# Two memory attentions of a two-block transformer kernel: probabilities normalised by GpSimd before they are turned, values stationary in the weighing

## The reference, cut to what matters

```python
def memory_attention(mq, mk, mv):
    sc = jnp.einsum('bshd,bmhd->bhsm', mq, mk, preferred_element_type=jnp.float32) * (MEM_HEAD_DIM ** -0.5)
    p = jax.nn.softmax(sc, axis=-1)
    out = jnp.einsum('bhsm,bmhd->bshd', p.astype(mv.dtype), mv)
    return out.reshape(B, S, MEM_W)
...
        mo = memory_attention(mq, mk, mv)
        x = x + jnp.concatenate([mixed, mo], axis=-1) @ w_out[l]
```

## Time and profile before

| what | value |
|---|---|
| median of 3 runs | 3211.76 us (3211.11 to 3211.96) |
| the profiled execution's own time | 3211.97 us |
| its span, first to last instruction | 3210.2 us |
| mean granted TensorE clock | 0.998 |
| PE busy | 3160.4 us, 98% |
| DVE busy | 1786.2 us, 56% |
| ACT busy | 1143.9 us, 36% |
| POOL busy | 430.5 us, 13% |

### The profile page before, as it was taken

How to read it: one execution, slowest core, us unless ns; L and a number is a source line. 1 busy time by engine, 2 the same in 40 slices (tenths; PEclk the granted TensorE clock), 3 DMA queues, 4 the chain that set the end, 5 groups by cost and what they waited for, 6 DMA issues and landing times. The chain is left out here.

```text
span 3210.2 us, 41446 instructions
## 1 busy us (share of the span) xinstructions
PE 3160.4 (98%) x15754; PEld 2584.8 (81%) x15754; DVE 1786.2 (56%) x1932; ACT 1143.9 (36%) x1331; POOL 430.5 (13%) x335
## 2 busy tenths in 40 slices
PE   8999999999999999999999999999999999999998
PEld 6778888877788888888877888888888877878887
DVE  7875635459653445534586754345444577664344
ACT  4553212259332222322343433223322343533221
POOL 0002000110100025000253120003000154120002
PEclk9999999999999999999999999999999999999999
DMA  4212232322122224232221122324223221122222
GB/s 158 83 47 99 92 105 92 107 96 83 69 92 92 95 101 122 89 108 92 92 80 66 62 89 86 105 90 131 92 92 104 79 92 67 53 94 93 102 94 76
DMA packets 46600, 293.45 MB, mean 91 GB/s; under 512 B 5888, under 2 KB 6272, under 8 KB 18336
## 3 DMA queue, kind: packets, MB, share of 16 engines
q1 hardware_dynamic: 44496, 286.97, 25.9%
q0 software_dynamic: 2000, 5.05, 1.0%
HBM read 289.24 MB, written 2.10 MB: 91 GB/s over the span
## 5 line engine op out<-in xcount | busy, mean ns | idle before, releaser
L1925 DVE TENSOR_TENSOR w_lo<-w_raw,w_hi 128x2048 fp32r<-128x2048 f32 (+1 forms) x284 | 667.0, 2349 | 244.1 <-ACT w_hi L1484 243.9
L903 PE MATMUL ps<-xg_hi,w_hi 128*128 128x512 f32 x1920 | 749.6, 390 | 2.2 <-DVE w_lo L1925 2.2
L903 PE MATMUL ps<-xg_hi,w_lo 128*128 128x512 f32 x1920 | 747.1, 389 | 0.0
L903 PE MATMUL ps<-xg_lo,w_hi 128*128 128x512 f32 x1920 | 747.0, 389 | 0.0
L1484 ACT ACTIVATE w_hi<-w_raw 128x2048 fp32r<-128x2048 f32 (+1 forms) x286 | 541.1, 1892 | 461.2 <-PE ps L903 359.5
L903 PE MATMUL ps<-hid_hi,w_hi 128*128 128x512 f32 x1216 | 473.3, 389 | 0.0
L903 PE MATMUL ps<-hid_lo,w_hi 128*128 128x512 f32 x1216 | 473.0, 389 | 0.0
L903 PE MATMUL ps<-hid_hi,w_lo 128*128 128x512 f32 x1216 | 473.0, 389 | 0.0
L903 PEld LDWEIGHTS ps<-xg_hi,w_hi 128*128 128x128 f32 x1920 | 360.4, 188 | 79.2 <-issue 4.8
L903 PEld LDWEIGHTS ps<-xg_lo,w_hi 128*128 128x128 f32 x1920 | 360.5, 188 | 75.8 <-issue 1.4
L903 PEld LDWEIGHTS ps<-xg_hi,w_lo 128*128 128x128 f32 x1920 | 360.4, 188 | 75.3
(11 more groups left out here) (369 smaller groups left out, 3902.4 us busy)
## 6 DMA issues: line engine op xcount, KB each, us to landing
w_raw<-up_dram SPq DMA_DIRECT2D x120, 1024.0 KB, 4.8
w_raw<-in_dram SPq DMA_DIRECT2D x42, 1024.0 KB, 4.9
w_raw<-down_dram SPq DMA_DIRECT2D x32, 1024.0 KB, 4.8
w_raw<-down_dram SPq DMA_DIRECT2D x32, 768.0 KB, 4.2
w_raw<-down_dram SPq DMA_DIRECT2D x32, 640.0 KB, 3.9
w_raw<-out_dram SPq DMA_DIRECT2D x14, 1024.0 KB, 4.8
w_raw<-out_dram SPq DMA_DIRECT2D x8, 768.0 KB, 4.2
w_raw<-memk_dram SPq DMA_DIRECT2D x4, 1024.0 KB, 4.9
```

The costliest lines, as they stand in the source:

```text
L903: last = pe.matmul(to, (w_hi, w_lo)[wp][:, q, t:t + P], parts[xp], start=(k == 0 and m == 0), stop=(k == p.ktiles - 1 and m == 2))
L1925: dve.tensor_tensor(w_lo[:, q, 0:w], w_raw[:, q, 0:w], w_hi[:, q, 0:w].bitcast(F32), ALU.subtract)\
```

## The change

For both memory attentions: DVE takes the reciprocal of unit n+1's row sums at its unit n (`inverse_memory`), POOL multiplies the exponentials by it in place, one instruction per head (`normalise`), and only then does PE turn them. The weighing has the values stationary and the turned probabilities moving (`weigh_memory`), so that its output has features on the partitions; DVE takes `hi` and `lo` from there (`finish_memory`). `turn_out` and the multiplication of `back` are gone for memory units. The near attention of the second block keeps the old steps; only its semaphore counts move. `rec` is one buffer, so the next reciprocal waits until POOL has used the last.

```diff
+WINDOWS = 16
+MEMORIES = 12
...
+        def normalise(u):
+
+            pool.wait_ge(rec_done, u.n + 1)
+            s_ = score_sb(u)
+            for i in range(u.nh):
+                last = pool.tensor_scalar(s_[:, i, :], s_[:, i, :], rec[:, i:i + 1], None, ALU.mult)
+            last.then_inc(norm_done, 1)
...
+        for u in SECTIONS["window"][WINDOWS:]:
+            normalise(u)
+
         for p in PHASES:
+            if p.name == "in1_1":
+                for u in M1:
+                    normalise(u)
...
         def turn_probs(u):
-            pe.wait_ge(exp_done, u.n + 1)
+            if u.kind == "memory":
+                pe.wait_ge(norm_done, u.n + 1 - WINDOWS)
+            else:
+                pe.wait_ge(exp_done, u.n + 1)
...
+        def weigh_memory(u):
+            pe.wait_ge(pt_ready, u.n + 1)
+            pe.wait_ge(ot_ready, u.f)
+            for i in range(u.nh):
+                for kb in range(u.nk):
+                    last = pe.matmul(ps[:, u.o_bank, i * P:(i + 1) * P], u.v[kb][i], turned(u)[:, kb, i * P:(i + 1) * P],
+                                     start=(kb == 0), stop=(kb == u.nk - 1))
+            last.then_inc(o_psum, 1)
...
-                if n and us[n - 1].kind == "memory":
-                    turn_out(us[n - 1])
                 if n in MEM_UNITS:
                     memory_slab(MEM_UNITS.index(n))
                 if u.kind == "window":
                     weigh_window(u)
                 else:
-                    weigh(u)
+                    weigh_memory(u)
...
-            first_out(1, 4, 6)
-            turn_out(us[-1])
-            first_out(1, 6, 8)
+            first_out(1, 4, 8)
...
-                if n:
-                    turn_out(M1[n - 1])
                 if 1 <= n < 7:
                     out_half(n - 1)
-                weigh(u)
+                weigh_memory(u)
             out_half(6)
-            turn_out(M1[-1])
             out_half(7)
...
+        def inverse_memory(u):
+            dve.wait_ge(exp_done, u.n + 1)
+            if u.n > WINDOWS:
+                dve.wait_ge(norm_done, u.n - WINDOWS)
+            dve.reciprocal(rec[:, 0:u.nh], rowsum[:, u.n % 2, 0:u.nh]).then_inc(rec_done, 1)
+
+        def finish_memory(u):
+            dve.wait_ge(o_psum, u.n + 1)
+            o = ps[:, u.o_bank, 0:u.nh * P].rearrange("p (t q) -> p t q", t=u.nh)
+            dve.tensor_copy(u.hi[0], o).then_inc(o_ready, 1)
+            dve.wait_ge(o_ready, u.n + 1)
+            dve.tensor_tensor(u.lo[0], o, u.hi[0].bitcast(F32), ALU.subtract).then_inc(ot_ready, 1)
...
         def attention(us):
...
                 if u.kind == "window":
                     finish_window(u)
                     if us[n + 1].kind == "window":
                         inverse_window(us[n + 1])
+                    else:
+                        inverse_memory(us[n + 1])
                 else:
-                    back(u)
-                    if n and us[n - 1].kind != "window" and us[n - 1].last:
-                        finish(us[n - 1])
+                    if n + 1 < len(us):
+                        inverse_memory(us[n + 1])
+                    finish_memory(u)
...
                 output(n)
+            inverse_memory(M1[0])
             front(M1[1], 1)
             low(DT - 1)
             split(MIX_O + 1)
...
                 if n == 2:
                     split(MIX_O + 2)
-                back(u)
-                if n:
-                    finish(M1[n - 1])
-            finish(M1[-1])
+                if n + 1 < len(M1):
+                    inverse_memory(M1[n + 1])
+                finish_memory(u)
```

More of the change, by code:

```diff
@@ L372, in program @@
     rec_done = sem("rec_done")
+    norm_done = sem("norm_done")
     o_ready = sem("o_ready")
@@ L2154, in finish_window @@
             dve.tensor_tensor(u.lo, o, u.hi.bitcast(F32), ALU.subtract).then_inc(ot_ready, 1)
+        def inverse_memory(u):
[9 more added lines that the diff above has]
+            dve.tensor_tensor(u.lo[0], o, u.hi[0].bitcast(F32), ALU.subtract).then_inc(ot_ready, 1)
         def back(u):
             dve.wait_ge(exp_done, u.n + 1)
+            if u.n == WINDOWS + MEMORIES:
+                dve.wait_ge(norm_done, MEMORIES)
             dve.reciprocal(rec[:, 0:u.nh], rowsum[:, u.n % 2, 0:u.nh]).then_inc(rec_done, 1)
@@ L2173, in finish @@
         def finish(u, between=None):
-            dve.wait_ge(ot_psum, u.f + 1)
+            dve.wait_ge(ot_psum, u.f + 1 - MEMORIES)
             src = ps[:, u.ot_bank, u.ot_col:u.ot_col + u.ntile * P]
[L2177 to L2194, removed]
-        def attention(us):
[L2197 to L2201, removed]
+            parts = [(src[:, t * P:(t + 1) * P], u.hi[t], u.lo[t],
+                      v("na_gain", 4 * (u.nf // NCB) + t)) for t in range(4)]
+            for s_, hi, lo, g in parts:
+                last = dve.tensor_scalar(hi, s_, g, None, ALU.mult)
+            last.then_inc(ot_hi, 1)
+            if between is not None:
+                between()
+            dve.wait_ge(ot_hi, u.f + 1 - MEMORIES)
+            for s_, hi, lo, g in parts:
+                last = dve.scalar_tensor_tensor(out=lo, in0=s_, scalar=g, in1=hi.bitcast(F32), op0=ALU.mult,
+                                                op1=ALU.subtract)
+            last.then_inc(ot_ready, 1)
+        def attention(us):
+            inverse_window(us[0])
             for n, u in enumerate(us):
@@ L2204, in attention @@
                     front(us[n + 2], n + 2)
-                if us is SECTIONS["window"] and n in MEM_AHEAD:
+                if n in MEM_AHEAD:
                     split = MEM_SLAB + MEM_AHEAD[n]
                     split_low(split, split % 2, SLAB_T * P)
-                if us is SECTIONS["window"] and n in MEM_UNITS:
+                if n in MEM_UNITS:
                     memory_slab(MEM_UNITS.index(n))
@@ L2213, in attention @@
                         inverse_window(us[n + 1])
-                else:
-                    back(u)
-                    if n and us[n - 1].kind != "window" and us[n - 1].last:
-                        finish(us[n - 1])
-                if us is SECTIONS["window"] and n in MEM_SPLITS:
+                    else:
+                        inverse_memory(us[n + 1])
+                else:
+                    if n + 1 < len(us):
+                        inverse_memory(us[n + 1])
+                    finish_memory(u)
+                if n in MEM_SPLITS:
                     split = MEM_SLAB + MEM_SPLITS[n]
                     split_low(split, split % 2, SLAB_T * P)
-            finish(us[-1])
         rope_n = [0]
```

## The result

| | before | after |
|---|---|---|
| median | 3211.86 us (3210.29 to 3212.23, 6 runs) | 3237.52 us (3236.12 to 3239.39, 6 runs) |
| the profiled execution's own time | 3211.97 us | 3236.64 us |
| its span | 3210.2 us | 3234.8 us |
| granted TensorE clock, mean | 0.998 | 0.996 |

The changed kernel takes 1.0081 of the time before (95% interval 1.007 to 1.0092): 25.7 us more, where 3.7 were forecast. The sign is the forecast's; the time is 15.7 us past the upper end of its range. The profiled executions alone lie 24.7 us apart.

A forecast was written before the change was run, and what follows sets the result against it. PE, busy in 98% of the span, was taken to bound the kernel. Added waits less removed transposes and waits gave +1.9 us in layer 0 and +1.75 in layer 1: 3211.76 + 3.7 = 3215.5 us, range 3211.5 to 3221.8.

The forecast's parts named there:

- the upper end of its range: 3221.8 us: 0.55 us per POOL head gives +8.0, and one meeting or one clock fall +2.
- Where time passes: In both layers' memory units, PE's turning waits for DVE's reciprocal and POOL's multiplications; the first waits +3.55 and +2.8 us.
- the turning of unit 16: Layer 0: reciprocal behind unit 15's closing, then POOL; turning starts at 231.15, not 227.60, +3.55 us, with no filling.
- The loop of layer 1: Turning to next turning takes 4.13 us against 3.47 of PE's own work: +0.65 in units 2, 4, 5, 6.
- The unit with the split: Layer 1, unit 3: DVE's split of 2.29 us stands between front(4) and its reciprocal, +2.85 us.
- the lower end of the range: 3211.5 us: 0.30 per head gives +2.4, PE's fewer changes between groups -1.2, and 1 us for the layout.
- The removed part: The 32 output transposes on PE, their waits and changeovers: 8 to 10 us gained if nothing took their place.
- POOL's price: POOL's multiplications, per 128x256 head: 0.343 us apart, 0.40 for the last; 1.43 us for 4 heads, 0.74 for 2.
- The rival of long heads: POOL's heads in both stretches take longer, each 0.1 us costing 2.2 us; at 0.69, 3223.2 us. Chance 0.20.
- The meeting with a split: POOL work meeting a DVE low split: counted on the slower side, with +2 for one meeting or clock fall.
- +2: Allowance in us at the range's upper end for one meeting with a split or one clock fall.
- The clock: Rival: PE's clock falls after idling 3.55, 2.8 and 2.85 us in one piece. Chance 0.07, half beyond 0.2%.

The follow-up runs named there:

- e1_two_op: The changed kernel with a second operation, times 1.0, added to POOL's multiplication; 3220.28 us, ratio 1.0028 to the kernel before.
- e9_early_two_op: The changed kernel with DVE's reciprocal of unit n+1 ahead of front(n+2) and POOL's multiplication given a second operation, times 1.0; 3208.47 us.
- e10_short_splits: The changed kernel with the two low splits behind units 16 and 17 cut to 128 of 2048 columns; 3231.76 us.
- e6_own_rec: The changed kernel with memory reciprocals in their own buffer, ahead of front(n+2), and unit 16's ahead of unit 15's closing; 3207.18 us.
- e5_filled_less: The changed kernel with 22, 18, 14, 13 and 14 unread identity products in PE's gaps ahead of five turnings; 3229.75 us.

## Why the prediction was wrong

**Where time passes: right.** The whole price is exposed waiting of PE at the turnings behind the chain scores, front, reciprocal, POOL, and unit 16 has no cover. Put 0.91 for 0.343 into the forecast's own chain and its places come out: the turning of unit 16 at +3.55 and 2.21 (four heads at 3.64 less 1.43), 5.76; measured 233.58 against 227.60, 5.98, of which the stretch began 0.35 late. The loop of layer 1 at 4.13 + 1.08 = 5.21 us; measured 5.23 from 863.84 to 869.07, and 5.59 in the unit before. The unit with the split 4.13 + 2.2 + 1.08 = 7.41; measured 844.31 to 851.73, 7.42. One side sum of the forecast doesn't come out: its own terms for the lower end of the range, +2.4 - 1.2 - 1, give 3212.0 us, not 3211.5. Nothing hangs on it.

**The removed part: right.** 8 to 10 us forecast, 9.3 measured.

**POOL's price: the step that failed.** The forecast said "The nearest rows are the same operation on 512 columns". It was not the same: L725 has two scalars, and the row's name, TENSOR_SCALAR, hides that; the source line shows it. Half of 0.69 was a fair guess for the two-scalar form (0.46 apart measured, 0.11 more), and the row of copies gave the price of a copy, while the form in the diff took 0.92, above the "from above 0.69" that was to bound it. By the forecast's units, 2.21 us for each of units 16 to 18 and 1.08 for each of units 1 to 6 of layer 1 are +13.1 us. The rival of long heads had this mechanism and the right side, at 0.20; it gave 3223.2 us at its 0.69, and its slope of 2.2 us per 0.1 us leads to 3228 at 0.92.

**The meeting with a split: left out, and it came twice.** The forecast's sum, with short heads, holds no meeting, and the upper end of its range allows for one. With long heads POOL's groups of units 17 and 18 both run into a split and take 1.6 us more each, +3.2 us. A head of 0.92 or 0.48 us that began inside a split of 2.28 or 2.40 came out at 2.5 (2.55, and 2.51 in e1_two_op), and no head was longer than 0.93 once the split was short. A head already at work when the split began did not hold the split up: 0.93 and 2.28 us (246.23 and 246.61 above). The "+2" that the range has for one meeting or one clock fall was the author's estimate, and no run shows it as one price; the runs showed 1.6 us for a meeting here (2.0 in e1_two_op, 3.88 less 1.85) and, by the rows, 1.4 to 1.7 for a fall.

**The clock: put at 0.07, and it fell four times.** Gaps of 5.56, 4.49, 3.40 and 3.60 us were followed by turnings and scores slower by, in order, 0.9 + 0.7, 0.2 + 1.5, 0.5 + 0.9 and 0.5 + 0.9 us: 6.1 us by these rows, 7.8 by the filled gaps and medians. The forecast's argument against it, full clock where PE waits now (granted 1.00 from 227 to 262 and from 817 to 853 us of the kernel before), rested on waits of at most 1.2 us in these stretches and said nothing of gaps three times as long. Whether its own gaps of 3.55, 2.8 and 2.85 would have brought a fall is open, but 0.07 was low. In e1_two_op a fall came after 3.77 us at unit 16, and one soon after the turning that ended a gap of 2.71 us in layer 1:

```profile
839.18 0.66 PE L1054 MATMUL ps<-ident,sc_m 128*128 128x128 f32 x4 [2.71 <-POOL sc_m L702]
839.67 1.55 PE L1040 MATMUL ps<-mk,proj 128*128 128x256 f32 x4
```

None came after 2.66 us there (unit 1 of layer 1, whose scores took 1.03).

The sum with these: 3.7 + 13.1 + 3.2 + 6.1 + 0.5 = 26.6 us, the last for unit 0 of layer 1, whose turning waited for POOL too (its weight loads stand 0.53 us behind POOL at 831.88). Measured were 25.7 by medians and 24.7 in the profiled executions, so the parts are together 1 to 2 us too large. The three errors hang together: with POOL's forecast price the groups would mostly have ended before the splits (with two scalars, 0.46 apart, one still met one), and the gaps would have been shorter. The range was built from each end by itself, so it held none of the compounded cases.

## What to carry to other kernels

Before pricing an instruction by a row of the same name, read the source line of that row: count of scalars and operations belong to the form, and here one of each on GpSimd took nearly twice the time of two of each (0.92 against 0.48 us). Where work of another engine goes onto TensorE's path, ask first whether its starting signal can be given earlier: here that was worth more (23.6 us) than the cheaper form (16.5). And price a new gap of several microseconds with the slower matmuls that may stand behind it: here 1.4 to 1.7 us behind four of the five gaps of 3.4 to 5.6.

## What the runs showed of the hardware

- A GpSimd tensor_scalar on 128x256 float32 took 0.92 us with one scalar and one operation, and 0.48 with a second operation, times 1.0, added.
- A GpSimd head that began inside a low split of DVE (`w_lo<-w_raw,w_hi`, 128x2048, 2.28 us) took 2.55 rather than 0.93 us; one already at work when the split began took 0.93.
- TensorE's matmuls behind some gaps ran for a few microseconds at a granted clock of 0.50 (234 to 236 and 251 to 253 us in the changed kernel, 1.00 again from 237 and 254): the scores of two heads took 1.91 us against 1.03. The length of the gap alone doesn't tell whether this came. It came after 3.40 and 3.60 us in layer 1, after the 3.77 us of unit 16 in e1_two_op and e9_early_two_op (scores of four heads 3.38 and 3.52 against 1.89), and in e1_two_op after 2.71 (two heads 1.55 against 1.03); it did not after 3.62 us at unit 18 of the changed kernel (turning 1.09, granted 1.00), nor after 2.86 at unit 17 of e10_short_splits (scores 1.89). What decides between these was not tried.
- Executions of one program differ in it: e6_own_rec's fell into three groups some 2 us apart, with mean clocks of 0.999, 0.998 and 0.997.
- Identity products that nobody reads, put into the gaps, took 7.8 us off the median and left all executions of e5_filled_less at a mean clock of 0.998.
